# The small experts' phases from unit 16 in place of unit 20 of a mixture of experts, and their tokens' gather one part of units earlier

## The reference

```
logits = xt @ w_router                      # 256 tokens, 8 experts
top_v, top_i = lax.top_k(logits, 2)
comb = softmax of top_v, at top_i, else 0
for e in range(8):
    y = y + comb[:, e:e + 1] * ((silu(xt @ wg[e]) * (xt @ wu[e])) @ wd[e])   # 1024 -> 3584 -> 1024
```

## Time and profile before

| | us |
|---|---|
| median of 3 runs | 1703.5 |
| lowest and highest | 1701.96, 1704.08 |
| the profiled execution, as timed | 1704.3 |
| its span in the profile | 1702.5 |
| PE busy | 1662.7 (98%) |
| DVE busy | 1187.8 (70%) |
| ACT busy | 977.7 (57%) |

### The profile page before, as it was taken

One profiled execution on the slowest core, in us unless ns is written; L12 is line 12 of the kernel. 1 busy time (PEld: TensorE's weight loads), 2 busy tenths in 40 slices (PEclk: granted clock), 3 DMA queues, 4 the chain that ended last, 5 costly groups with the idle time before them and its releaser, 6 DMA issues.

```text
span 1702.5 us, 22772 instructions
## 1 busy us (share of the span) xinstructions
PE 1662.7 (98%) x8809; PEld 1332.5 (78%) x8809; DVE 1187.8 (70%) x1338; ACT 977.7 (57%) x1189; POOL 124.8 (7%) x210
## 2 busy tenths in 40 slices
PE   7999999999999999999999999999999999999998
PEld 7988888898877766776677677766887897878886
DVE  8865454588777775767577577766998897755555
ACT  5644444455666664665566466645777666654564
POOL 0000000000683000000000000000001001000000
PEclk9999999999899999999999999999999999999999
DMA  9555555546589999999999999999999744345421
GB/s 334 160 195 185 189 192 191 180 149 210 195 333 398 411 414 408 410 378 412 410 407 411 413 407 411 395 400 411 413 354 380 274 166 152 125 135 165 147 100 38
DMA packets 148570, 487.76 MB, mean 286 GB/s; under 512 B 13461, under 2 KB 14692, under 8 KB 134132
## 3 DMA queue, kind: packets, MB, share of 16 engines
q1 hardware_dynamic: 146496, 480.02, 74.8%
q0 software_dynamic: 1328, 4.72, 1.0%
q10 hardware_dynamic: 644, 1.63, 0.3%
HBM read 482.67 MB, written 3.67 MB: 286 GB/s over the span
## 4 chain that ended last, share of the span: by engine, by line
PE 80%; DMA 8%; DVE 8%; ACT 2%; issue 2%; POOL 0%; SPq 0%; POOLq 0%; DVEq 0%; ACTq 0%
PE ps L2110 67%; DVE wlo L1298 4%; DMA raw<-in_moe_w_up 4%; PE ps L2406 3%; DMA raw<-in_moe_w_gate 3%; PE ps L2420 2%; ACT whi L726 1%; PE ps L2520 1%; DVE arena L1288 1%; DVE arena L1782 1%; DMA raw<-in_moe_w_down 1%; PE ps L2368 0%; PE ps L2369 0%; PE ps L2254 0%; PE ps L2202 0%
## 5 line engine op out<-in xcount | busy, mean ns | idle before, releaser
L1298 DVE TENSOR_TENSOR wlo<-raw,whi 128x1024 fp32r<-128x1024 f32 x742 | 870.2, 1220 | 395.8 <-ACT whi L726 394.3
L726 ACT ACTIVATE whi<-raw 128x1024 fp32r<-128x1024 f32 x742 | 744.1, 1052 | 562.8 <-PE ps L2110 341.4
L2110 PE MATMUL ps<-whi,ya 128*128 128x512 f32 x1824 | 575.1, 392 | 2.8 <-issue 1.2
L2110 PEld LDWEIGHTS ps<-whi,ya 128*128 128x128 f32 x1824 | 342.7, 188 | 80.5 <-issue 7.6
L2110 PE MATMUL ps<-wlo,ya 128*128 128x512 f32 x912 | 355.3, 390 | 0.0
L2110 PE MATMUL ps<-whi,yh 128*128 128x512 f32 x672 | 213.6, 392 | 2.0 <-DVE wlo L1298 2.0
L2110 PEld LDWEIGHTS ps<-wlo,ya 128*128 128x128 f32 x912 | 171.4, 188 | 34.1
L2110 PE MATMUL ps<-hhi,whi 128*128 128x256 f32 x656 | 188.3, 287 | 1.9 <-DVE hlo L1360 1.5
L2110 PE MATMUL ps<-hlo,whi 128*128 128x256 f32 x656 | 185.6, 283 | 0.0
L2110 PE MATMUL ps<-hhi,wlo 128*128 128x256 f32 x656 | 185.6, 283 | 0.0
L2110 PEld LDWEIGHTS ps<-whi,yh 128*128 128x128 f32 x672 | 126.2, 188 | 32.2 <-issue 3.2
(11 more groups left out here) (428 smaller groups left out, 1322.3 us busy)
## 6 DMA issues: line engine op xcount, KB each, us to landing
raw<-in_moe_w_gate SPq DMA_DIRECT2D x112, 1024.0 KB, 10.0
raw<-in_moe_w_up SPq DMA_DIRECT2D x112, 1024.0 KB, 10.6
raw<-in_moe_w_down SPq DMA_DIRECT2D x112, 1024.0 KB, 10.2
raw<-in_even_w_in SPq DMA_DIRECT2D x21, 1024.0 KB, 5.2
raw<-in_w_in SPq DMA_DIRECT2D x20, 1024.0 KB, 6.0
raw<-in_odd_w_in SPq DMA_DIRECT2D x16, 1024.0 KB, 5.3
raw<-in_ffn_w_gate SPq DMA_DIRECT2D x14, 1024.0 KB, 5.1
raw<-in_ffn_w_up SPq DMA_DIRECT2D x14, 1024.0 KB, 5.1
```

The costliest lines, as they stand in the source:

```text
L726: act.activation(hi_of(u)[:, n], raw[:, k % RAW, n], ACT.Copy).then_inc(w_hi, 1)
L1298: dve.tensor_tensor(lo_of(u)[:, n], raw[:, k % RAW, n], hi_of(u)[:, n].bitcast(F32), ALU.subtract).then_inc(w_lo, 1)
L2110: ins = pe.matmul(o, s, m, start=first and n == 0, stop=last and n == 2, skip_group_check=True)
```

## The change

```diff
-FIRST_PHASE, PHASE_SPACING = 20, 9.0
+FIRST_PHASE, PHASE_SPACING = 16, 9.2
@@ ACT, small()
-                if here in ((0, 1, "g"), (0, 1, "u")):
-                    small_gath(here[2] == "u")
+                if here in ((0, 0, "u"), (0, 1, "g")):
+                    small_gath(here[2] == "g")
@@ DVE, run()
                     after(u0 + up[n][0], d, len(up[n]))
+                    if n == 0 and not loop and j == 0:
+                        small_onehot()
                     used(u0 + up[n][-1], d)
                     hid(j, n)
-                    if n == 0 and not loop and j == 0:
-                        small_onehot()
@@ PE, small()
-                if here in ((0, 1, "g"), (0, 1, "u")):
-                    small_gather(here[2] == "u")
+                if here in ((0, 0, "u"), (0, 1, "g")):
+                    small_gather(here[2] == "g")
```

## The result

| | before | after |
|---|---|---|
| median of 10 runs each, us | 1703.8 | 1707.4 |
| ratio of the times, with 95% interval | | 1.0023 [1.0014, 1.0031] |
| the profiled execution's span, us | 1702.5 | 1705.5 |
| phase 0 begins, us | 500.60 | 496.31 |
| phase 20 begins, us | 1176.57 | 1179.61 |

The changed kernel is slower by 3.7 us in the medians. The forecast was 1708.1 us, slower by 4.6 us. The sign, the size and the mechanism came out; the terms inside the sum did not all, as will be seen. First the page of the changed kernel, the lines that answer.

A forecast was written before the change was run, and what follows sets the result against it. PE bounds the kernel, with DMA loads almost equally long from 504.3 to 1190 us. 1703.5 + 5.2 (wait for the one-hot) - 1.8 (waits for loads) + 1.2 (clock) = 1708.1 us; range 1702.6 to 1710.8 us.

The forecast's parts named there:

- Part 1, the hole: At the gather's first half behind unit 7, PE idles 5.2 us for DVE's one-hot; all four engines shift by that.
- Part 2: Phase 0 after 16 units in place of 20 begins at 495.0 us, with no wait for its four loads.
- Part 3, the spacing: Between phase 0 and phase 20, the new phase spacing shrinks PE's waits for loads by 1.8 us.
- the list of work minus loads: Per interval between phases, PE's work minus DMA's load time; negative entries, taken as waits, total 11.5 us before, 9.7 after.
- the sentence on the TURNs: Behind phases 3, 9 and 15, TURNs get four units' cover, two of them had two; at most part of the 1.8 us.
- Part 4, the clock: Behind PE's hole the clock falls, costing 1.2 us, from a range of 0 to 1.8 us.
- the two rows that I took: Clock prices from slow transposes after the idle program start, 1.8 us, and slow gather instructions ahead of unit 0, 0.9 us.
- The clock holds: Behind PE's hole the clock does not fall: 1706.9 us; chance 0.25.
- The new spacing gives nothing: From phase 0 on, DMA stalls move with the units, so no load waits are saved: 1710 to 1710.5 us; chance 0.14.
- The hole is absorbed: Loads go on during PE's hole and later waits shrink by its 5.2 us: say 1702.7 us; chance 0.10.
- No hole: At unit 7 the one-hot is ready in time and phase 0 starts at 490 us: 1701.7 us; chance 0.08.

The follow-up runs named there:

- the phases alone: The kernel before with only FIRST_PHASE, PHASE_SPACING changed to 16, 9.2, gather and one-hot at their old places: 1707.4 us, ratio 1.0022 to the kernel before.
- the gather alone: The changed kernel with FIRST_PHASE, PHASE_SPACING back at 20, 9.0, so only gather and one-hot stand earlier: 1710.7 us, ratio 1.0040 to the kernel before.
- PE kept busy: The changed kernel with 44 unused transposes on PE ahead of its wait for the one-hot: 1704.4 us, ratio 1.0002 to the kernel before.
- the phases alone with the copy moved: The kernel before with phases at 16, 9.2 and ACT copying the gather's second half ahead of its splits of units 17 and 18: 1700.9 us, ratio 0.9985.
- one-hot first: The changed kernel with DVE's one-hot ahead of the splits of units 7 to 10: 1700.3 us, ratio 0.9980 to the kernel before.
- the same with the old phases: The changed kernel with DVE's one-hot ahead of the splits of units 7 to 10 and phases at 20, 9.0: 1703.6 us, ratio 1.0000 to the kernel before.
- the first experiment: The changed kernel with DVE's one-hot moved ahead of the splits of units 7 to 10, same run as one-hot first: 1700.3 us, ratio 0.9980.

## Why the prediction was right, and where its terms were not

**Part 1, the hole: right.** 5.2 us were forecast, from 463.1 to 468.3; 4.96 us came, from 463.0 to 468.0. The one-hot ran at 466.88 us, forecast 467.1. DVE's queue could be read off the kernel before, because nothing between the splits was to change. That all engines shift and the ring is full was right too: SP issues nothing from 467.3 to 478.2 us, and the DMA stands from 472 to 476 us. The gather's second half waited for nothing.

**Part 2: right.** Phase 0 was to begin at 495 to 496 us and began at 496.31 us without a wait for its loads. Its place rests on the earlier gather, though, as the phases alone showed, or on ACT's copy ahead of two splits.

**Part 3, the spacing: the total too small, for a step that failed.** 1.8 us of waits less were forecast, 3.1 came. The part that the list of work minus loads counts, waits for loads, shrank by 1.3 us between these two traces and by 2.0 us on average over all of them, so the 1.8 us are about right. The failed step is the sentence on the TURNs, that more cover for them "takes away at most what is in the -1.8 already". It wasn't in it: the TURN's wait of 1.35 us for DVE (the row at 617.48 us above) is no wait for a load. It left because phase 3 changed from an up part to a gate part, and with that both the TURN's cover and the product's place in DVE's order; the order alone was shown to be enough. I had summed all waits of the window of the earlier trace rows, 10.8 us, compared them with the 11.5 us of my list and called the rule good. It was a coincidence of sums: only 9.0 of the 10.8 us were what the list counts. The table of PE's waits over that stretch, which I had not set beside the list, has the 1.4 us in a row of its own. Nor does the list fit place by place: it has 1.2 us of wait from phase 11 to 12 and 0.4 us from 12 to 13, and the trace has none and 1.47 us.

One reading of the prediction is wrong without harm. It says that PE hardly waits after 1190 us; the third row has 150.00 - 147.03 = 3.0 us, 2.0% of the stretch, where the middle has 1.6%. Most of these waits are for DVE (L1288 and L1298), and they are in both traces.

**Part 4, the clock: right in kind, under-sized.** I took 1.2 us between 0.9 and 1.8; 1.7 us came in the changed kernel, near the dearer bound, and 2.7 us behind the same hole in the gather alone, above it. So the two rows that I took weren't bounds. In the changed kernel the hole ended in 16 short instructions that PE took at 0.50, all of them and not the first nine. That the trace agrees with what the Trainium skill says of an idle array (TensorE: Matmul & The Clock Gate, Part 1: The HAM clock gate) is now shown by the 0.50 behind three holes, of 4.96, 4.96 and 5.55 us.

**The errors cancelled in part.** In the changed kernel the forecast terms give +4.6 us, the measured ones 5.0 + 1.7 - 3.1 = 3.6 us. The clock's price was 0.5 us too low, the hole's 0.2 us too high, and the new spacing's gain 1.3 us too small. That the total came within 1 us of the measured 3.7 owes something to luck.

**The rivals.** *The clock holds* falls by the 0.50 in three traces, and PE kept busy gives 1.5 us back. *The new spacing gives nothing* falls by the phases alone with the copy moved (0.9985) and by one-hot first against the same with the old phases (0.9980 against 1.0000). *The hole is absorbed* falls by the gather alone, 1.0040, and by SP, which issues no load from 467.3 to 478.2 us in the changed kernel. The rule of the Trainium skill that would bring it about (DMA: Bandwidth & Descriptors, Where 436 GB/s comes from) isn't borne out here, with one core running: 405 to 407 GB/s are held for more than 680 us. *No hole* is what the first experiment built; its 1700.3 us are below the 1701.7 us of that rival, by about the 1.4 us of the TURN's wait, which its sum hadn't either.

## What to carry to other kernels

Ahead of moving a consumer earlier, read in its producer's queue when the input will be made. The edit that brings the input forward must go ahead of the work that fills that queue: ahead of `hid` it was worth about 1.1 us by the rows of before (an estimate, not tried alone), ahead of the eight split halves 5.0 us and the clock. When a rule is fitted to a total of waits, take the total apart by what was waited for first; a sum that fits within 1 us had a wait of another kind in it. And take more than one trace where waits of 1 to 2 us are compared: one pair showed 1.3 us less, nine traces 2.0 us. And an order on an engine that is harmless at one place (ACT's copy behind two splits, DVE's product behind one) becomes a wait of up to 5.6 us when the loads behind a phase are what those splits wait for.

## What the runs showed of the hardware

- Behind a hole of 5.0 us on PE the granted clock is 0.50 in place of 1.00, and it came back while PE worked on. The cost was 1.7 us in the changed kernel, 2.7 us behind the same hole in the gather alone, and 2.3 us in the phases alone (hole 5.55 us, the phase 9.38 in place of 7.09 us). The waits for loads of up to 1.8 us lie in a stretch whose mean stays at 1.00. Work whose result nobody uses held the clock at 1.00 through the same 5 us.
- The DMA held 405 to 407 GB/s for more than 680 us with one core running, and 412 GB/s from 463 to 468 us, with PE standing (the changed kernel) as with PE busy (one-hot first).
